# The two heads of a pair taken in turn on TensorE, in the logits and in the value product of a hybrid decoder layer

## What is computed

```
def fox_attend(q, k, v, cq, ck, q_pos, k_pos):
    s = einsum('nqhd,nkhd->nhqk', q, k) * (HEAD_DIM_A ** -0.5)
    s = s + cq[..., None] - ck[..., None, :]       # cumulative log of the forget gates
    s = where(k_pos[None, :] <= q_pos[:, None], s, -inf)
    p = softmax(s, axis=-1)
    return einsum('nhqk,nkhd->nqhd', p, v)

def hybrid_layer(x, p, ...):
    x = x + 0.5 * swiglu(rms_norm(x, ...), ...)
    h = rms_norm(x, p['mix_norm'])
    q, k, v, f, bx_in, by_in, sb, sc, sx, g = split_columns(h @ p['w_in'])
    o_a = attn_fn(rms_norm(q), rms_norm(k), v, log_sigmoid(f + b_forget))
    ...                                            # o_b, o_c: the two other mixers
    x = x + (gates[0] * (o_a @ wb_a) + gates[1] * (o_b @ wb_b) + gates[2] * (o_c @ wb_c)) @ p['w_out']
    return x + 0.5 * swiglu(rms_norm(x, ...), ...)
```

## Time and profile before

| | |
|---|---|
| executions | 3121.61, 3118.79, 3120.39 us |
| span of the profiled execution, first to last instruction | 3121.0 us |
| TensorE busy | 96% of the span, 21632 matmuls |
| VectorE, ScalarE busy | 47%, 32% |
| mean granted TensorE clock | 0.978 |

### The profile page before, as it was taken

The page is one execution under the profiler, slowest core; times in us unless marked ns, Lnnn a source line. Parts: engine busy times, 40 slices in busy tenths (PEclk is TensorE's granted clock), DMA queues, the critical chain, the costliest instruction groups (busy, mean ns, idle before and its releaser), DMA issues.

```text
span 3121.0 us, 54813 instructions
## 1 busy us (share of the span) xinstructions
PE 2990.7 (96%) x21632; PEld 2892.3 (93%) x21632; DVE 1465.1 (47%) x2025; ACT 992.6 (32%) x1287; POOL 104.4 (3%) x104
## 2 busy tenths in 40 slices
PE   7999998999999999999999999989999999999998
PEld 7999998888899999999999999988889999999998
DVE  4434345555745443343443333466565544433334
ACT  4211123444533332211231212324445333312123
POOL 1000001000000000000000000100000001000001
PEclk9999999999999999999999999999999999999999
DMA  3222222333222222222222222222332222222222
GB/s 114 79 82 81 79 64 82 83 81 81 70 87 81 85 81 80 82 67 81 69 82 68 95 68 81 81 64 79 80 81 89 80 82 88 81 68 81 81 78 74
DMA packets 299022, 248.82 MB, mean 80 GB/s; under 512 B 20643, under 2 KB 296307, under 8 KB 298919
## 3 DMA queue, kind: packets, MB, share of 16 engines
q1 hardware_dynamic: 296775, 242.44, 25.4%
q0 software_dynamic: 2144, 4.98, 0.5%
HBM read 240.04 MB, written 7.34 MB: 79 GB/s over the span
## 4 chain that ended last, share of the span: by engine, by line
PE 89%; DVE 4%; ACT 2%; issue 2%; DVEq 1%; DMA 0%; POOLq 0%; ACTq 0%; SPq 0%
PE ps L448 81%; PE ps L609 2%; PE ps L664 1%; ACT whi L752 1%; DVE wlo L1006 1%; PE ps L693 1%; PE ps L587 0%; PE ps L610 0%; DVE tmp L1012 0%; DVEq L1046 0%; PE ps L654 0%; PE ps L596 0%; ACT hh L771 0%; DVE x L1023 0%; PE ps L640 0%
## 5 line engine op out<-in xcount | busy, mean ns | idle before, releaser
L1006 DVE TENSOR_TENSOR wlo<-wraw,whi 128x1024 fp32r<-128x1024 f32 (+1 forms) x456 | 548.9, 1206 | 1351.9 <-ACT whi L752 1349.4
L448 PE MATMUL ps<-hh,whi 128*128 128x288 f32 x4480 | 968.9, 298 | 18.8 <-ACT vtok L850 6.1
L448 PE MATMUL ps<-hl,whi 128*128 128x288 f32 x4480 | 962.9, 297 | 0.0
L448 PE MATMUL ps<-hh,wlo 128*128 128x288 f32 x4480 | 961.9, 296 | 0.0
L752 ACT ACTIVATE whi<-wraw 128x1024 fp32r<-128x1024 f32 (+1 forms) x456 | 474.6, 1043 | 1460.1 <-PE ps L448 1409.0
L448 PEld LDWEIGHTS ps<-hh,whi 128*128 128x128 f32 x4480 | 725.4, 190 | 25.5 <-ACT vtok L850 6.3
L448 PEld LDWEIGHTS ps<-hl,whi 128*128 128x128 f32 x4480 | 725.7, 190 | 0.0
L448 PEld LDWEIGHTS ps<-hh,wlo 128*128 128x128 f32 x4480 | 724.9, 189 | 0.0
L448 PE MATMUL ps<-ah,whi 128*128 128x288 f32 x1408 | 313.8, 306 | 72.5 <-DVE al L1052 72.5
L448 PE MATMUL ps<-al,whi 128*128 128x288 f32 x1408 | 311.1, 304 | 0.0
L448 PE MATMUL ps<-ah,wlo 128*128 128x288 f32 x1408 | 309.8, 302 | 0.0
(11 more groups left out here) (282 smaller groups left out, 2503.5 us busy)
## 6 DMA issues: line engine op xcount, KB each, us to landing
wraw<-in_ffn_w_in SPq DMA_DIRECT2D x88, 1024.0 KB
wraw<-in_ffn_w_out SPq DMA_DIRECT2D x32, 1024.0 KB
wraw<-in_w_in SPq DMA_DIRECT2D x28, 1024.0 KB
wraw<-in_w_in SPq DMA_DIRECT2D x56, 512.0 KB
wraw<-in_ffn_w_out SPq DMA_DIRECT2D x16, 768.0 KB
wraw<-in_w_branch SPq DMA_DIRECT2D x24, 512.0 KB
wraw<-in_w_out SPq DMA_DIRECT2D x9, 1024.0 KB
kv<-in_cache_k SPq DMA_DIRECT2D x128, 64.0 KB, 1.9
```

Source lines behind the costliest of these rows:

```text
L448: last = pe.matmul(ps[slot][:, half, 0:HF], weights, rhs[:, k, half * HF:(half + 1) * HF], start=(start and c == 0 and n == 0), stop=(stop ...
L1006: dve.tensor_tensor(split_tile(wlo, j, rowwise), raw_tile(slot, j, rowwise), split_tile(whi, j, rowwise).bitcast(F32), ALU.subtract).then_ ...
```

## The change

The logits loop now goes over halves of the query blocks, and within a query block it issues each kind of matmul for head 0 and then for head 1. The two float32 matmuls use different halves of TensorE's rows. Uses 9 and 11 are filled in the first half, 10 and 12 in the second (before: 9, 10, 11, 12). The transposes of head 1's probabilities come directly after the projection of use 20. Both value products come at the end, issued in turn for each key block; they write different halves of TensorE's columns. A second buffer for transposed probabilities is laid over columns 768 to 2047 of `kpt`, whose cached keys have been used by then; the semaphore `pv_done` is gone. ScalarE's order of instructions, VectorE's, and the DMA queues are as before.

```
@@ -198,7 +198,7 @@
                 kv = sb("kv", [P, SB * NPG, P], F32, m2)
                 kpt = sb("kpt", [P, SB * PAST], F32, m2)
                 prob = [sb(f"prob{i}", [P, 10 * P], F32, m2) for i in range(2)]
-                probt = sb("probt", [P, 10 * P], F32, m2)
+                probt = [sb("probt", [P, 10 * P], F32, m2), kpt[:, 6 * P:16 * P]]
                 probs = sb("probs", [P, 3 * P], F32, m2)
                 probst = sb("probst", [P, 3 * P], F32, m2)
                 qp = sb("qp", [P, N], F32, m2)
@@ -251,7 +251,7 @@
         qk_squared, qk_ready = sem("qk_squared"), sem("qk_ready")
         xc_ready = sem("xc_ready")
         max_ready, exp_ready, prob_ready = sem("max_ready"), sem("exp_ready"), sem("prob_ready")
-        pv_done, vp_ready = sem("pv_done"), sem("vp_ready")
+        vp_ready = sem("vp_ready")
         gates_ready, root_in, root_ready = sem("gates_ready"), sem("root_in"), sem("root_ready")
         f_ready = sem("f_ready")
         oh_ready, o_ready = sem("oh_ready"), sem("o_ready")
@@ -597,20 +597,23 @@
                         last.then_inc(filled[pr.slot(k)], 1)
 
                     pe.wait_ge(qk_ready, it + 1)
-                    for e in range(2):
-                        for qb in range(QB):
-                            k = 9 + 2 * e + qb // 2
-                            if qb % 2 == 0:
-                                wait_psum(pr, k, L, p)
+                    for half in range(2):
+
+                        for e in range(2):
+                            wait_psum(pr, 9 + 2 * e + half, L, p)
+                        for qb in (2 * half, 2 * half + 1):
                             n = (qb + 1) * P
-                            out = ps[pr.slot(k)][:, qb % 2, :]
-                            hs = slice(HD * e, HD * (e + 1))
+                            outs = [ps[pr.slot(9 + 2 * e + half)][:, qb % 2, :] for e in range(2)]
                             qs = slice(qb * P, (qb + 1) * P)
-                            pe.matmul(out[:, 0:n], qp[hs, qs], kp[hs, 0:n], start=True, stop=False)
-                            pe.matmul(out[:, 0:n], cq[e][:, qs], ck[:, 0:n], start=False, stop=False)
-                            last = pe.matmul(out[:, qb * P:n], identb[:], maskd[:], start=False, stop=True)
-                            if qb % 2:
-                                last.then_inc(filled[pr.slot(k)], 1)
+                            for e in range(2):
+                                hs = slice(HD * e, HD * (e + 1))
+                                pe.matmul(outs[e][:, 0:n], qp[hs, qs], kp[hs, 0:n], start=True, stop=False)
+                            for e in range(2):
+                                pe.matmul(outs[e][:, 0:n], cq[e][:, qs], ck[:, 0:n], start=False, stop=False)
+                            for e in range(2):
+                                last = pe.matmul(outs[e][:, qb * P:n], identb[:], maskd[:], start=False, stop=True)
+                                if qb % 2:
+                                    last.then_inc(filled[pr.slot(9 + 2 * e + half)], 1)
 
                     wait_psum(pr, 13, L, p)
 
@@ -656,14 +659,16 @@
                             if kb % 2:
                                 last.then_inc(filled[pr.slot(k)], 1)
 
-                    def weighted(e):
-
-                        k = (18, 23)[e]
-                        pe.wait_ge(freed[pr.slot(k)], pr.turn(k, L, p) + 1)
+                    def weighted():
+
+                        for k in (18, 23):
+                            pe.wait_ge(freed[pr.slot(k)], pr.turn(k, L, p) + 1)
                         for kb in range(QB):
-                            last = pe.matmul(ps[pr.slot(21)][HD * e:HD * (e + 1), 0, kb * P:SEQ], vp[:, kb, HD * e:HD * (e + 1)],
-                                             probt[:, koffs[kb]:koffs[kb] + (QB - kb) * P], start=(kb == 0), stop=(kb == QB - 1),
-                                             skip_group_check=True)
+
+                            for e in range(2):
+                                last = pe.matmul(ps[pr.slot(21)][HD * e:HD * (e + 1), 0, kb * P:SEQ], vp[:, kb, HD * e:HD * (e + 1)],
+                                                 probt[e][:, koffs[kb]:koffs[kb] + (QB - kb) * P], start=(kb == 0), stop=(kb == QB - 1),
+                                                 skip_group_check=True)
                         return last
 
                     transposed(0, 17)
@@ -678,10 +683,9 @@
                     project(pr.slot(20), 6, range(4), hh, hl, stop=False)
                     wait_weights(pr, 7, L, p)
                     project(pr.slot(20), 7, range(4, KD), hh, hl, start=False).then_inc(filled[pr.slot(20)], 1)
+                    transposed(1, 22)
                     pe.wait_ge(vp_ready, it + 1)
                     wait_psum(pr, 21, L, p)
-                    weighted(0).then_inc(pv_done, 1)
-                    transposed(1, 22)
 
                     pe.wait_ge(freed[pr.slot(19)], pr.turn(19, L, p) + 1)
                     pe.wait_ge(kv_loaded, it * 512 + 512)
@@ -692,7 +696,7 @@
                         for g in range(NPG):
                             pe.matmul(out[:, rs], kv[:, s * NPG + g, :], probst[:, g * P + 16 * s:g * P + 16 * s + 16],
                                       start=False, stop=(s == SB - 1 and g == NPG - 1), skip_group_check=True)
-                    weighted(1).then_inc(filled[pr.slot(21)], 1)
+                    weighted().then_inc(filled[pr.slot(21)], 1)
 
 
                 st = S["state"]
@@ -914,19 +918,19 @@
                     act.drain()
                     act.activation(tmp[4][:, 0:XB], tmp[0][:, 0:XB], ACT.Square).then_inc(gates_ready, 1)
 
-                    def copy_pt(k0):
+                    def copy_pt(e, k0):
                         for kb in range(QB):
                             k = k0 + kb // 2
                             if kb % 2 == 0:
                                 wait_tile(pr, k, L, p)
                             w = (QB - kb) * P
                             off = (0, 4 * P, 7 * P, 9 * P)[kb]
-                            ins = act.activation(probt[:, off:off + w], ps[pr.slot(k)][:, kb % 2, 0:w], ACT.Copy)
+                            ins = act.activation(probt[e][:, off:off + w], ps[pr.slot(k)][:, kb % 2, 0:w], ACT.Copy)
                             if kb == 1:
                                 ins.then_inc(free(k), 1)
                         ins.then_inc(free(k0 + 1), 1)
 
-                    copy_pt(17)
+                    copy_pt(0, 17)
 
                     act.wait_ge(by_ready, it + 1)
                     wait_tile(pr, 19, L, p)
@@ -938,8 +942,7 @@
                     split_ahead(pr, 6, 20, L, p)
                     split_ahead(pr, 7, 20, L, p)
 
-                    act.wait_ge(pv_done, it + 1)
-                    copy_pt(22)
+                    copy_pt(1, 22)
 
                     wait_tile(pr, 21, L, p)
                     op = o[:, bass.ds(p, 1), :].rearrange("p a n -> p (a n)")
```

## The result

The changed kernel took 3124.97 us (median of 20 executions, 3119.32 to 3131.8), the kernel before in the same comparison 3120.55 (20 executions, 3115.27 to 3126.35). The ratio is 1.0015, with a 95% interval of 1.0008 to 1.0022: slower by 4.4 us, clear of the noise but inside the 0.2% that the prediction counted as no change.

What follows compares the result with a forecast made beforehand. TensorE, with 89% of the chain, was taken as the bound. Fixed gain -10.3, clock at value products +2.0, clock after the logits' stall +9.6, idle after fourth pairs +2.1: +3.4 on 3121.0, so 3124.4 us; range 3116 to 3129.

Steps and rivals of the forecast that it cites:

- The logits take 4.94 us.: Logits of both heads on TensorE: row halves overlap fully, 4.94 us instead of 8.17, a saving of 3.23 a pair.
- The wait for `ps1`, 0.49, and the wait for use 9, 2.5, leaving 0.28.: Around the logits: start 0.49 us late, then a 2.5 us stall before the sample's logits; 0.28 us a pair remains saved.
- The end of the turn, 1.34 us earlier and a wait of 1.0.: Value products start 1.34 us earlier, after a 1.0 us stall on ScalarE's copy; lost in the fourth pair.
- Both heads in the time of one product.: Value products on two column halves overlap: both heads take 2.30 us at 2.4 GHz, as one did.
- The clock after the new wait.: After the stall behind the logits: clock falls in seven in ten of 8 turns, 1.7 us each, +9.6 us.
- The clock at the value products.: Value products of pairs 1 to 3: clock falls cost 1.9 us a pair, 11.4 instead of 9.4, +2.0 us.
- Idle time after the fourth pair, +2.1.: After each layer's fourth pair: TensorE's idle time grows from 1.56 to about 2.9 us, lowering its clock, +2.1 us.
- the holding clock (1): Rival: clock does not fall after the logits' stall or after the fourth pair; 3112 us, chance 0.30.
- That the row halves do not overlap (2): Rival at the logits: head 0's last mask 2.13 us later, half of the other falls kept; 3134 us, chance 0.14.

Runs made afterwards that it cites:

- version by halves: Changed kernel with VectorE's maxima and ScalarE's exponentials of the logits taken by halves of the query blocks, giving use 9 back earlier: 3095.41 us, ratio 0.9919 against before.
- end of the turn alone: Changed kernel with the logits in the order of before, so only the new end of the turn remains: 3115.10 us, ratio 0.9981 against before.
- filled version: Changed kernel with 40 unused 128-column bf16 matmuls ahead of head 1's last mask, where TensorE would idle: 3114.51 us, ratio 0.9978 against before.

## Why the prediction was right

- **The logits take 4.94 us.** Right: in the version by halves, where nothing is waited for behind them, it is 4.83 us from their start to the sample's.
- **The wait for `ps1`, 0.49, and the wait for use 9, 2.5, leaving 0.28.** 0.43 and 2.40; start of the sample's logits 7.39 us after the logits' start, where the steps gave 7.40. From the key transposes (L596, at 567.98) to the sample's logits it is 9.73 us, before 10.01: the 0.28. The version by halves shows that the wait is use 9's and nothing else's.
- **The end of the turn, 1.34 us earlier and a wait of 1.0.** Right: a wait of 1.04 us, released by the copy, and in the end of the turn alone the value products start 33.70 us after the logits, before 35.03. The end of the turn alone gave -6.4 us where 8.0 less some clock was summed.
- **Both heads in the time of one product.** Right: 2.30 us at a clock of 1.00, so the weight loads, for which 0.19 to 0.5 us more was weighed, cost nothing extra.
- **The clock after the new wait.** The mechanism was right and its size too small: eight falls, not seven in ten of eight at 1.7; by the filled version 12.6 us in all, and not 9.6 (the sum's own factors give 9.5).
- **The clock at the value products.** Mis-sized the other way: in the profiled execution pairs 1 to 3 took 9.7 us over 2.30, against 9.2 before; +0.5 and not +2.0.
- **Idle time after the fourth pair, +2.1.** Wrong. It did not grow: the fourth product itself ran at 1.2 GHz and used up the time (L706 waits 1.9 us in its two turns together, L702 before 3.1), and no fall followed the wait. The sum had used the same time twice: once to hide pair 4's slower value product, and once more as idle time that would lower the clock.

With these sizes the sum is -10.3 + 12.6 + 0.5 + 0 = +2.8, against +3.4 predicted and +4.4 in the medians. That the total came so near is in part luck: one term was 3.0 too small, two others 1.5 and 2.1 too large. Over the loop the two profiled executions differ by +1.8 us (264.4 and 264.3 us a layer from the first logits to L706, before 263.5 and 263.4 to L702). The six turns that are not a layer's last come out even, 0.1 us longer in all: there what the new order saves and what the falls cost cancel. The two last turns are 0.8 to 0.9 longer each.

The profiled execution of the changed kernel is 3 us under the median, and outside the loop it is 2.7 us shorter than the one before, with 112.6 us at 1.2 GHz there against 119.5. Single executions of either kernel spread over some 11 to 12.5 us; whether the clock outside the loop makes that spread was not seen, since one execution of each kernel was profiled. So the loop, as profiled, shows less than half of the 4.4 us by which the medians differ, and where the rest lies is open.

Of the rivals, the holding clock (1) is what the filled version builds: 3114.5, where 3112 was worked out. That the row halves do not overlap (2) was worked out at 3134, and the kernel built that way took 3137.6, with the sample's logits 1.97 us later than in the changed kernel, where the rival had 2.13. But the rival kept half of the falls behind the logits; those were gone, and two longer ones stood within the logits, so the nearness of the totals is luck.

## What to carry to other kernels

Before two streams are interleaved on one engine, follow which buffer the next step waits for: interleaving finishes both streams late, so whoever consumes "all of stream 0" starts late, and the gain can become a wait of the same size. Make the consumers follow the new order of filling (here 2.56 us a turn), and then look at the granted clock: at the place seen here an idle stretch of 2.4 us cost up to another 1.6, and unused work in the gap gave most of that back.

## What the runs showed of the hardware

- Float32 matmuls on the two row halves, issued one after the other, ran fully side by side (1.06 us for 512 columns, two or four records), and so did those on the two column halves (2.30 us).
- Waits of 2.4 us after the logits went with a fall to 0.50 in all 16 turns of two kernels, waits of 1.0 us there in none of 6, and no wait (or 0.2 us) there in none of 16 turns of the version by halves and the filled one.
- The clock can fall without an idle stretch just ahead: in two of eight turns within logits on one row half at a time.
- A fall that is avoided at one place can return at the next: with the wait after the logits filled, the time at 1.2 GHz at the end of the turn grew from 30.7 to 47.0 us over eight turns.
